# The wkv7 chunk loop: a 64-token block inverse with a two-step solve among the next chunk's levels

## What is computed

```python
def step(S, inp):
    r_t, w_t, k_t, v_t, a_t, b_t = inp
    Sa = jnp.einsum("bhij,bhj->bhi", S, a_t)
    S = S * w_t[:, :, None, :] + Sa[..., None] * b_t[:, :, None, :] + v_t[..., None] * k_t[:, :, None, :]
    return S, jnp.einsum("bhij,bhj->bhi", S, r_t)
```

## Time and profile before

| | |
|---|---|
| median of 3 runs | 3219.44 us (3219.29 to 3223.38) |
| the profiled execution | 3221.72 us, span 3220.1 us, mean granted TensorE clock 0.957 |
| TensorE matmuls | 2980.5 us busy, 93%, 19,177 instructions |
| VectorE / ScalarE / GpSimd | 1455.8 / 683.0 / 341.7 us busy |
| HBM | 205 MB read, 40 MB written |

### The profile page before, as it was taken

How to read it: one execution, slowest core, us unless ns; L and a number is a source line. 1 busy time by engine, 2 the same in 40 slices (tenths; PEclk the granted TensorE clock), 3 DMA queues, 4 the chain that set the end, 5 groups by cost and what they waited for, 6 DMA issues and landing times.

```text
span 3220.1 us, 47602 instructions
## 1 busy us (share of the span) xinstructions
PE 2980.5 (93%) x19177; PEld 2747.1 (85%) x19177; DVE 1455.8 (45%) x1504; ACT 683.0 (21%) x1015; POOL 341.7 (11%) x322
## 2 busy tenths in 40 slices
PE   6999999999999999798878989835999999999998
PEld 6999999999999999634368888713899999999998
DVE  3332332235738877745444444456544332332233
ACT  4110111113112233223222222101222110111113
POOL 0000000000012311200035444200000000000000
PEclk8999999999999999899988999976899999999999
DMA  3111111113244566854500000010421111111112
GB/s 99 46 46 47 46 44 53 46 41 117 93 124 126 182 210 197 301 181 123 158 9 1 1 1 1 13 26 13 145 92 47 46 46 46 46 46 52 46 39 72
DMA packets 264334, 246.77 MB, mean 77 GB/s; under 512 B 17364, under 2 KB 212784, under 8 KB 264064
## 3 DMA queue, kind: packets, MB, share of 16 engines
q1 hardware_dynamic: 247040, 184.09, 19.2%
q0 software_dynamic: 16960, 60.66, 5.1%
q10 hardware_dynamic: 192, 0.07, 0.0%
HBM read 204.95 MB, written 39.82 MB: 76 GB/s over the span
## 4 chain that ended last, share of the span: by engine, by line
PE 87%; DVE 9%; ACT 2%; issue 1%; DMA 0%; DVEq 0%; POOL 0%; SPq 0%; POOLq 0%; ACTq 0%
PE ps L1541 65%; PE ps L1857 3%; PE ps L1748 3%; PE ps L1875 3%; PE ps L1873 2%; PE ps L1564 1%; DVE rstd L1454 1%; PE ps L1921 1%; PE ps L1585 1%; PE ps L1766 1%; DVE small L1351 1%; DVE chunk_work L1396 1%; PE ps L1793 1%; PE ps L1781 1%; DVE chunk_work L1393 1%
## 5 line engine op out<-in xcount | busy, mean ns | idle before, releaser
L1541 PE MATMUL ps<-h_hi,w_hi 128*128 128x344 f32 x3072 | 991.8, 323 | 10.3 <-DVE w_lo L1075 10.3
L1541 PE MATMUL ps<-h_lo,w_hi 128*128 128x344 f32 x3072 | 980.6, 319 | 0.0
L1541 PE MATMUL ps<-h_hi,w_lo 128*128 128x344 f32 x3072 | 980.2, 319 | 0.0
L1541 PEld LDWEIGHTS ps<-h_hi,w_hi 128*128 128x128 f32 x3072 | 577.7, 188 | 25.9 <-issue 19.8
L1541 PEld LDWEIGHTS ps<-h_lo,w_hi 128*128 128x128 f32 x3072 | 578.0, 188 | 2.1 <-issue 1.9
L1541 PEld LDWEIGHTS ps<-h_hi,w_lo 128*128 128x128 f32 x3072 | 578.0, 188 | 0.0
L1541 PE MATMUL ps<-ff_hi,w_hi 128*128 128x344 f32 x1056 | 337.1, 319 | 0.0
L1541 PE MATMUL ps<-ff_lo,w_hi 128*128 128x344 f32 x1056 | 336.6, 319 | 0.0
L1541 PE MATMUL ps<-ff_hi,w_lo 128*128 128x344 f32 x1056 | 336.2, 318 | 0.0
L744 ACT ACTIVATE w_hi<-w_stage 128x1024 fp32r<-128x1024 f32 x194 | 203.8, 1051 | 479.8 <-PE ps L1541 479.8
L1075 DVE TENSOR_TENSOR w_lo<-w_stage,w_hi 128x1024 fp32r<-128x1024 f32 x194 | 239.2, 1233 | 138.0 <-ACT w_hi L744 103.7
(11 more groups left out here) (390 smaller groups left out, 3746.0 us busy)
## 6 DMA issues: line engine op xcount, KB each, us to landing
w_stage<-in_ffn_up SPq DMA_DIRECT2D x176, 256.0 KB, 3.1
key_ring<-in_cache_k SPq DMA_DIRECT2D x128, 256.0 KB, 3.0
value_ring<-in_cache_v SPq DMA_DIRECT2D x128, 256.0 KB, 2.9
w_stage<-in_w_in SPq DMA_DIRECT2D x84, 256.0 KB, 3.3
w_stage<-in_ffn_down SPq DMA_DIRECT2D x80, 256.0 KB, 2.9
gate_save<-tmp POOLq DMA_DIRECT2D x16, 516.0 KB, 4.5
gate_ring<-gate_save POOLq DMA_DIRECT2D x16, 516.0 KB, 4.2
x_save<-x_res POOLq DMA_DIRECT2D x8, 516.0 KB, 2.9
```

Source lines behind the costliest of these rows:

```text
L1541: last = mm(dense[s][:, j], w[w0][:, k0 + k, :], r[:, k, j * CH:(j + 1) * CH], start=(k == 0 and n == 0), stop=(k == nk - 1 and n == 2))
```

## The change

The inverse is now built in 64-token diagonal blocks: five levels (4 to 64). Both blocks of a matrix lie in one compact 128x64 tile (tokens 0 to 63 of the block on partitions 0 to 63, tokens 64 to 127 on the others), so both halves x of a quantity are one 128x512 tile and one instruction on VectorE, ScalarE and GpSimd. TensorE's products of a level are 64x64 by 64x64, alternating between the quadrants of the array (rows and columns 0 to 63, rows and columns 64 to 127); T1, DX and DY have one PSUM bank each. The solve goes in two steps: U of the first 64 tokens, then R of the last 64 is corrected by the cross block LO times that U, then U of the last 64. R, U, state and outputs of chunk c-1 stand among the levels of chunk c; there is a ninth round with the solve alone. The blocks of chunk c+1 stand between the lower product and the corrections of level 3. Constants of the loop are 64 columns wide except two; X, Y and btm have two buffers, T1, R, U, LO and LT one. The reciprocal L1417 comes between levels 2 and 3 of chunk 0 on VectorE.

The diff, cut to its core:

```diff
-LEVELS = 6
+LEVELS = 5
...
+        T1_PS, DX_PS, DY_PS, U_PS = [by_head(b) for b in (0, 1, 2, 7)]
+        R_PS, LO_PS, L_PS, ABA_PS = [two_banks(b, n) for b, n in ((3, 0), (3, 256), (5, 0), (5, 256))]
+        AKA_PS, AKR_PS, ABR_PS = [PS[:, b:b + 2, :].rearrange("p x (h n) -> p x h n", h=HP) for b in (5, 3, 5)]
+        TOK_PS = [ps4(7, 0, C), ps4(7, 0, C), ps4(3, 0, C)]
+        DS_PS, Y_PS = ps4(3), ps4(4, 0, C)
...
# GpSimd
+            gram_sides(0)
+            keys(0)
+            queries(0)
+            first_masks(0)
             for c in range(NC):
+                if c + 1 < NC:
+                    gram_sides(c + 1)
+                mask(c, 2)
+                if c + 1 < NC:
+                    keys(c + 1)
+                mask(c, 3)
+                mask(c, 4)
+                if c + 1 < NC:
+                    queries(c + 1)
+                    first_masks(c + 1)
...
# ScalarE
+            for c in range(NC + 1):
+                p = c - 1
+                if c < NC:
+                    t1_move(c, 0)
+                if c:
+                    act.wait_ge(*ev.at("ck_r", p + 1))
+                    sc.activation(Rs, R_PS, ACT.Copy).then_inc(ev["ck_r_moved"], 1)
+                    solution(p, 0)
+                if c < NC:
+                    t1_move(c, 1)
+                    act.wait_ge(*ev.at("ck_lo", c + 1))
+                    sc.activation(LO[halves[0]], LO_PS[halves[0]], ACT.Copy).then_inc(ev["ck_lo_moved"], 1)
+                if c:
+                    solution(p, 1)
+                if c < NC:
+                    t1_move(c, 2)
+                if c:
+                    act.wait_ge(*ev.at("ck_y", p + 1))
+                    sc.activation(CUM[:, :, p * C:(p + 1) * C], Y_PS, ACT.Copy).then_inc(ev["ck_y_out"], 1)
+                if c < NC:
+                    t1_move(c, 3)
+                    move(c, 0, vtok)
+                    t1_move(c, 4)
+                    move(c, 1, ktok)
+                    move(c, 2, btok)
+                if c + 2 < NC:
+                    decays(c + 2)
...
# VectorE
+                if c < NC:
+                    level_sums(c, 0)
+                    dve.wait_ge(*ev.at("ck_aka_made", c + 1))
+                    in_turn(v.tensor_tensor(heads8(aka), heads8(AKA_PS), wide("strict"), ALU.mult).then_inc(ev["ck_aka"], 1))
+                if c:
+                    full_side(p)
+                if c < NC:
+                    level_sums(c, 1)
+                    level_sums(c, 2)
+                if c:
+                    next_state(p)
+                else:
                     dve.wait_ge(*ev.at("o_root", 1))
                     in_turn(v.reciprocal(rmix[0:HP], rmix[0:HP]).then_inc(ev["o_rstd"], 1))
+                if c < NC:
+                    level_sums(c, 3)
+                    if c + 1 < NC:
+                        blocks(c + 1)
+                    dve.wait_ge(*ev.at("ck_akr_made", c + 1))
+                    in_turn(v.tensor_tensor(heads8(akr), heads8(AKR_PS), wide("incl"), ALU.mult).then_inc(ev["ck_akr"], 1))
+                    level_sums(c, 4)
+                    dve.wait_ge(*ev.at("ck_abr_made", c + 1))
+                    in_turn(v.tensor_tensor(heads8(arb), heads8(ABR_PS), wide("incl"), ALU.mult).then_inc(ev["ck_arb"], 1))
...
# TensorE
+            def lower_products(c, l):
...
+                for a in range(2):
+                    for h in range(HP):
+                        for q in halves:
+                            last = mm(T1_PS[q, a, h], m[q, a, h], x[q, a, h], start=True, stop=True)
...
+            def solve(p, q):
+
+                y = Ys[p % 2]
+                for x in range(2):
+                    for h in range(HP):
+                        last = mm(U_PS[q, x, h], y[q, x, h], Rs[q, x, h], start=True, stop=True)
```

More of the change, by code:

```diff
@@ new lines, in next_state @@
+            def next_state(p):
+                new = Ss[(p + 1) % 2]
+                dve.wait_ge(*ev.at("ck_ds", p + 1))
+                in_turn(v.tensor_tensor(new, Ss[p % 2], DS_PS, ALU.add))
+                in_turn(v.tensor_tensor(new, new, bc(span[:, :, p:p + 1], 64), ALU.mult).then_inc(ev["ck_s"], 1))
+            blocks(0)
+            for c in range(NC + 1):
+                p = c - 1
+                if c < NC:
[7 more added lines that the diff above has]
+                    level_sums(c, 2)
+                if c:
+                    next_state(p)
+                else:
@@ new lines, in level_products @@
+            def level_products(c, l):
+                y = Ys[c % 2]
+                pe.wait_ge(*ev.at("ck_t1_moved", level(c, l)))
+                if l == 0:
+                    pe.wait_ge(*ev.at("ck_y_first", c + 1))
+                if level(c, l) > 1:
+                    pe.wait_ge(*ev.at("ck_y_level", level(c, l) - 1))
+                if l < LEVELS - 1:
+                    for a in range(2):
+                        for h in range(HP):
+                            for q in halves:
+                                last = mm(DX_PS[q, a, h], y[q, a, h], T1s[q, a, h], start=True, stop=True)
+                    last.then_inc(ev["ck_dx"], 1)
+                for a in range(2):
+                    for h in range(HP):
+                        for q in halves:
+                            last = mm(DY_PS[q, a, h], T1s[q, a, h], y[q, a, h], start=True, stop=True)
+                last.then_inc(ev["ck_dy"], 1)
@@ new lines, in outputs @@
+            def outputs(p):
+                art, old = ar[p % 2], Ss[p % 2]
+                pe.wait_ge(*ev.at("ck_akr", p + 1))
+                pe.wait_ge(*ev.at("ck_arb", p + 1))
+                for h in range(HP):
+                    for x, q in enumerate(halves):
+                        mm(Y_PS[q, h], old[q, h, :], art[q, h, 1, :], start=(h == 0), stop=False)
+                for h in range(HP):
+                    for x, q in enumerate(halves):
+                        mm(Y_PS[q, h], vtok[:, h, q], akr[:, x, h], start=False, stop=False)
+                for h in range(HP):
+                    for x, q in enumerate(halves):
+                        last = mm(Y_PS[q, h], Us[:, x, h], arb[:, x, h], start=False, stop=(h == HP - 1))
+                last.then_inc(ev["ck_y"], 1)
@@ L1836, in _ @@
-                for h in range(HP):
-                    for x, q in enumerate(halves):
-                        last = mm(ABR_PS[x][:, h], bt[q, h, :], art[q, h, 1, :], start=True, stop=True)
-                last.then_inc(ev["ck_gram"], 1)
-                def turn(k, src):
-                    for h in range(HP):
-                        last = nc.tensor.transpose(TOK_PS[k][:, h], src[:, h], K("ident"))
-                    last.then_inc(ev["ck_tok"], 1)
-                pe.wait_ge(*ev.at("ck_ak", 2 * c + 2))
```

414 lines of the change are left out of this document (222 added, 192 removed).

## The result

| | us |
|---|---|
| before, median of 4 runs beside it | 3221.41 (3219.29 to 3224.47) |
| after, median of 4 runs | 3037.52 (3035.79 to 3041.41) |
| ratio | 0.943, 95% interval 0.9414 to 0.9446 |
| forecast | 3047, range 3025 to 3165 |
| profiled execution after | 3035.79, span 3034.1, mean granted clock 0.961 |

The change saves 184 us, where 172 had been forecast. In the other kernels some of these lines lie a few numbers off.

What follows compares the result with a forecast made beforehand. TensorE was taken to bound the loop: products 29.9 us plus shape changes 2.1 make 32.0; with waits of 0.6 to 0.9, 33 us a chunk against 56.4. The loop ends 172 us earlier: 3047 us, range 3025 to 3165.

Steps and rivals of the forecast that it cites:

- The bound: In the wkv7 loop, TensorE is followed without a gap for some 43 us of each 56.4 us chunk.
- 29 ns per instruction in two diagonal quadrants: Level products on TensorE: two streams of 58 ns run side by side, 29 ns each; 58 if one after another.
- The blocks: First products of a chunk on TensorE: 64 instructions at 29 ns; four quadrants at once would save 0.9 us a chunk.
- LU and LO: Substitution product and cross block on TensorE, after lower 1: 1.4 us together, covering the wait for the copy of T1.
- Changes of shape: TensorE's array changes shape 17 times a chunk, 3 already counted: 14 at 0.15 us, 2.1 us.
- Waits: TensorE's waits for copies and masks, including the third transposition for the AKR mask: 0.6 to 0.9 us a chunk.
- Chunk 0 and the end: At the loop's ends: the reciprocal puts the X sum off by about 3.5 us; the bare last solve takes 14.3 us.
- The clock: In the loop, each chunk's 6.8 us dip to 1.2 GHz goes with the head; if it stays, 27 us less gained, 3075.
- A: Level products: two quadrants writing the same PSUM bank don't run side by side, 58 ns each; 3144 us, chance 12%.
- B: TensorE's queue can't issue faster than about 55.5 ns per instruction in the loop; 3153 us, chance 10%.
- C: The array, a quarter filled by each product, falls to 1.2 GHz for the loop; 61 us slower, 3280 us, chance 6%.
- D: Filling fails: copies land behind other work on ScalarE and VectorE, levels stay bare; 38 us a chunk, 3082 us, chance 10%.

Runs made afterwards that it cites:

- The order experiment: Changed kernel with T1, DX and DY products issued one quadrant after the other instead of alternating: 3118.54 us, ratio 0.968.

## Why the prediction was right, and where its terms were off

The likeliest case came true, 10 us under its number and inside its own range.

**The bound.** Right. The experiment with DY twice shows that instructions on TensorE are what the time consists of (4.34 us for 160).

**29 ns per instruction in two diagonal quadrants.** Right, to the nanosecond: 0.93 us for 32. It was the term on which most hung (448 instructions a chunk), and it had been taken from a row with 64x64 weights and 128 moving columns and one with 64 moving columns, for want of a row with both. The order experiment shows the other end: with no alternation the same work costs 9.1 us more a chunk. By the upper bound of 58 it would have been 13.0: of the 3.9 between, 0.3 is the wait of the third transposition, which the slower groups cover, and the rest fits the seams.

**The blocks: the mis-sized term.** The prediction put their 64 instructions at 29 ns, 1.86 us, and named four streams as the other side of its range (0.9 less). They took 1.04: 0.8 us a chunk. The rule "two of 58 side by side" should have been carried on to four; the list of quadrants in the diff has four.

**LU and LO.** 0.93 for lower 1, 0.93 for LU and 0.46 for LO were added up to 2.3; it takes 1.92, since a group that stays in one quadrant overlaps its neighbours at the seams: 0.4 less.

**Changes of shape.** Priced at 0.15 each, 2.1 in all; found 1.9. The starts of the groups in a chunk give the single prices: 0.15 behind a lower product (1.08 us instead of 0.93) and behind a transposition (0.59 instead of 0.44), 0.19 behind a Gram group (1.09 instead of 0.90), 0.09 to 0.10 behind a half solve and behind DY of level 3, 0.05 at DX. So this term was right to 0.2.

**Waits.** 0.6 to 0.9 forecast, and the rounding up to 33 made it 1.0. Found 0.5: 0.33 for the AKR mask where it was named (1.41 us from DY to the transposition, 1.08 in the last chunk, where nothing holds it), 0.17 for the copy at level 4 (0.76 behind the transposition instead of 0.59). The four terms, 0.8 + 0.4 + 0.2 + 0.5, make 1.9 of the 2.03 us by which the period was off. All four were priced too high, so inside the period nothing cancels. The starts that these prices and waits are read from (timeline of TensorE, the changed kernel):

```profile
1746.51 0.66 PE L1975 MATMUL ps<-const,v_mix 128*128 128x128 f32 x4
1747.10 1.16 PE L1969 MATMUL ps<-chunk_work,chunk_work 64*128 64x128 f32 x16
1748.19 1.15 PE L1942 MATMUL ps<-chunk_work 64*64 64x64 f32 x32
1749.27 0.66 PE L1975 MATMUL ps<-const,chunk_work 128*128 128x128 f32 x4
1750.03 1.15 PE L1962 MATMUL ps<-chunk_work,chunk_work 64*64 64x64 f32 x32
1751.44 0.66 PE L1975 MATMUL ps<-const,chunk_work 128*128 128x128 f32 x4 [0.26 <-DVE chunk_work L1512]
```

**Chunk 0 and the end.** The reciprocal delayed the X sum, and TensorE waited 2.8 us, with 3.5 forecast. The bare solve took 16.4 us instead of 14.3, and the profile shows why: the last solve falls to half clock for 6.8 us, which the prediction had left out.

```profile
1883.40:1890.20 6.80, 5.62 (x52) 5.31 (x54) 0.75 (x2) 0.59 (x1) 0.00 (x0) 0.50 0.00 0
```

Together: seven periods −14.7, chunk 0 +0.9, end +2.1, so −11.7 us against the forecast: 184 saved instead of 172. Here the two ends took back 3.0 of what the periods gave.

**The clock.** The prediction let the dip of each chunk go with its head. Right for the chunks: from 1658.1 to 1883.4 there is none. The granted clock is 0.5 only at the loop's ends: until 1637.6, for 3.4 us behind the stall of the reciprocal, and in the last solve.

```profile
1658.10:1883.40 225.30, 220.19 (x5256) 205.77 (x5256) 96.56 (x127) 65.34 (x142) 90.75 (x72) 1.00 0.01 3
```

**The rivals.** A (the same PSUM bank puts the quadrants in series, 3144) fell with the first group of 32: T1, DX and DY of both diagonal quadrants write one bank, at 29 ns. The Trainium skill (TensorEngine Tiling, Restrictions and Gotchas) says that different row tiles can't access one bank at the same time; for diagonal quadrants the trace disagrees, and the measurement decides. B (an issue floor near 55 ns, 3153) fell too, with 15.6 ns on average over 64 starts. The Trainium skill (TensorE: Matmul & The Clock Gate, Part 1) names about 25 ns from start to start; the blocks stay below that figure as well. C (half clock for the loop, 3280) is excluded by the window above. D (the filling fails, 3082) is what the kernel without interleaving was to show; bare, the chunk costs 9.8 us more, not the 5 priced there: its waits are 4.5, and the clock adds some 4.

One count of the prediction was wrong, and nothing hangs on it: a chunk of the kernel before has 476 TensorE instructions, not 486.

## What to carry to other kernels

Small products pay when the instructions next to each other in TensorE's list use different quadrants: the order of the loops alone was worth 81 us here. Count the quadrants that a group touches in turn, two or four, and take the pace of one divided by it (shown here for 64x64 weights and 64 moving columns). Fill a wait on TensorE with independent work of the next stage even if the wait is short: with the solve bare, each chunk lost some 4 us to the lower clock beside 4.5 to waits. And before instructions are taken from such a list, ask which copy they were hiding.

## What the runs showed of the hardware that was not expected

- Four quadrants run side by side: 48 instructions in a row of 64x64 weights and 64 moving columns start every 14.6 ns, a quarter of the 58 of one quadrant (15.6 over the group's 64 starts).
- The overlap reaches only a few instructions ahead: when the quadrant changes once in 16 instructions, a seam hides about 0.17 us, three instructions' time, and the rest is serial.
- In the kernels with a bare solve, and in the last solve of the changed kernel, the granted clock fell to 0.5 for 6.8 to 13.7 us. It fell behind the first, second or third of the solve's four waits of 0.7 to 0.8 us, which have 1 us of one-quadrant products between them at the full clock; the other waits lie in the stretch. Waits of 0.3 (the changed kernel) or of 0.74, 0.28 and 0.39 in a chunk (the copy made twice) left it at 1.00. The last 18 us of the loop before, its bare solve among them, stood at the full clock too (1.00 from 2062 to 2080 us), with TensorE busy for 17.93 of 18.00 us.
- The times of one kernel spread by about 5 us, and the traces show one source of that size: the 500th product of TensorE starts anywhere from 107.2 to 112.3 us, in kernels that are the same up to there. The dips of the clock behind the loop fall differently too (the last mask to the last transposition took 52.5 us in one execution of the changed kernel and 55.0 in another), but that is made up behind it: from the last mask to the end both took 1194 us. A gain of 3 us is better read from the trace than from such medians.
